# RWKV scratch sized to the chunk, four masked state buffers in place of one, and the MLP down-projection with the token block outside

## What is computed

```
layer 0: x += concat(pool_mixer, rwkv7(12 heads x 64)) @ ev_w_out
         x += square(relu(rmsnorm(x) @ ff_w1[0])) @ ff_w2[0]      # 1024 -> 4096 -> 1024
layer 1: x += concat(gmlp, rglru) @ od_w_out
         x += square(relu(rmsnorm(x) @ ff_w1[1])) @ ff_w2[1]
y = rmsnorm(x)
rwkv7 step, per head: S = S*w - (S kk)(kk*a)^T + v k^T ;  o = S r   # S is 64 x 64, carried
```

## Time and profile before

| | us |
|---|---|
| median of 2 runs | 5295.91 (5283.2 and 5308.62) |
| the profiled execution | 5305.1 |
| its span, slowest core (core 4) | 5303.5 |
| spans of the 8 cores | 5230.9 to 5303.5 |

### The profile page before, as it was taken

How to read it: one execution, slowest core, us unless ns; L and a number is a source line. 1 busy time by engine, 2 the same in 40 slices (tenths; PEclk the granted TensorE clock), 3 DMA queues, 4 the chain that set the end, 5 groups by cost and what they waited for, 6 DMA issues and landing times.

```text
span 5303.5 us, 107077 instructions; the slowest of 8 cores (5230.9 to 5303.5 us)
## 1 busy us (share of the span) xinstructions
PE 4604.0 (87%) x32575; PEld 3193.8 (60%) x32575; DVE 2754.5 (52%) x7970; ACT 1622.8 (31%) x4545; POOL 1426.1 (27%) x3000
## 2 busy tenths in 40 slices
PE   6898889988899888988897987999977787799998
PEld 5676666766677666766665763444456565544445
DVE  4645655556465564565552223666554544456664
ACT  2323333333233332333332112111144444321112
POOL 3313232232222322233211210333323232123320
PEclk8998899999999989888998788999989898899999
DMA  5031130221301313013023033222356555412211
GB/s 79 3 55 21 25 53 1 30 48 25 53 1 25 53 17 61 1 25 49 4 40 59 5 50 88 33 33 33 44 65 77 68 75 70 63 29 33 33 17 66
DMA packets 341496, 213.11 MB, mean 40 GB/s; under 512 B 34738, under 2 KB 326433, under 8 KB 339912
## 3 DMA queue, kind: packets, MB, share of 16 engines
q0 software_dynamic: 294704, 160.98, 23.6%
q1 hardware_dynamic: 46232, 45.28, 2.8%
HBM read 345.84 MB, written 21.35 MB: 69 GB/s over the span
## 4 chain that ended last, share of the span: by engine, by line
PE 58%; DVE 16%; issue 9%; DMA 8%; ACT 6%; POOL 1%; SPq 1%; DVEq 1%; ACTq 0%; POOLq 0%
PE psb L451 46%; PE psb L550 10%; DVE arena L418 6%; DVE arena_r L418 5%; ACT arena_r L434 3%; DVE arena L426 3%; PE psb L454 2%; ACT arena L434 2%; DMA arena<-od_w_in 2%; DMA arena<-xin 2%; DMA arena<-ev_w_in 2%; POOL arena L418 1%; DVE arena L423 1%; ACT L434 1%; DMA o_wkv_s<-arena 1%
## 5 line engine op out<-in xcount | busy, mean ns | idle before, releaser
L451 PE MATMUL psb<-arena 128*128 128x512 bf16 (+12 forms) x17296 | 2740.7, 314 | 446.5 <-DVE arena L426 126.9
L451 PEld LDWEIGHTS psb<-arena 128*128 128x128 bf16 (+4 forms) x17296 | 1655.1, 140 | 1393.0 <-issue 937.5
L550 PE MATMUL psb<-arena 128*128 128x256 bf16 x11359 | 1617.5, 286 | 6.9 <-DVE arena L442 6.9
L550 PEld LDWEIGHTS psb<-arena 128*128 128x128 bf16 x11359 | 1118.3, 103 | 300.9 <-issue 110.3
L418 POOL TENSOR_TENSOR arena<-arena 128x128 f32<-128x128 f32 (+5 forms) x1421 | 751.9, 547 | 1490.6 <-ACT arena L434 519.9
L434 ACT ACTIVATE arena<-psb 128x512 f32<-128x512 f32 (+7 forms) x900 | 369.2, 424 | 1917.7 <-PE psb L451 1485.0
L418 DVE TENSOR_TENSOR arena<-arena,psb 128x512 f32<-128x512 f32 (+2 forms) x1427 | 700.6, 564 | 432.4 <-PE psb L451 426.8
L434 ACT ACTIVATE arena<-arena 128x128 f32<-128x128 f32 (+7 forms) x1792 | 531.9, 331 | 727.3 <-PE psb L451 317.4
L418 DVE TENSOR_TENSOR arena_r<-arena_r,psb 128x256 fp32r<-128x256 f32 x1248 | 480.4, 418 | 434.0 <-ACT arena_r L434 428.8
L426 DVE SCALAR_TENSOR_TENSOR arena<-arena 128x128 f32<-128x128 f32 (+6 forms) x1138 | 417.8, 408 | 352.4 <-ACT arena L434 338.1
L442 DVE COPY arena<-psb 128x256 f32<-128x256 f32 (+7 forms) x663 | 243.9, 374 | 659.1 <-PE psb L451 280.4
(11 more groups left out here) (22 smaller groups left out, 1046.3 us busy)
## 6 DMA issues: line engine op xcount, KB each, us to landing
arena<-ev_w_in POOLq DMA_DIRECT2D x99, 512.0 KB, 11.1
arena<-od_w_in POOLq DMA_DIRECT2D x72, 512.0 KB, 10.9
arena<-ff_w POOLq DMA_DIRECT2D x64, 512.0 KB, 5.7
arena<-ev_w_out POOLq DMA_DIRECT2D x36, 512.0 KB, 8.3
arena<-od_w_out POOLq DMA_DIRECT2D x36, 512.0 KB, 16.1
arena<-xscr SPq DMA_DIRECT2D x8, 1056.0 KB, 14.7
arena<-xin SPq DMA_DIRECT2D x16, 512.0 KB, 8.0
xscr<-arena SPq DMA_DIRECT2D x64, 128.0 KB, 7.1
```

Source lines behind the costliest of these rows:

```text
L451: return self._op("pe", lambda e: e.matmul(out, lhsT, rhs, start=start, stop=stop), R, W, "mm", cost=cost, rows=rows)
L550: K.P.filler = lambda: K.P.make_filler(lambda e: e.matmul(f_out, f_l, f_r, start=True, stop=True), fdep)
```

## The change

Three edits. In `rwkv` the scratch tiles are as long as the chunk (`n`) and no longer 128 columns; for prompt chunks `n` is 128, so only the sample chunk (`n` = 64) differs. The sample chunk gets four buffers `UVm` that are used in turn. In the down-projection of the MLP the token block becomes the outer loop and the output tile the inner one.

```diff
@@ ffn_all
             wb2 = wtile(2, 1024, w2[c * 256:(c + 1) * 256, :].rearrange("(k p) c -> p k c", p=128))
-            for m in range(8):
-                for (t0, tn) in TBS:
+            for (t0, tn) in TBS:
+                for m in range(8):
                     ps = K.ps()
                     for k in range(2):
@@ rwkv
-        XS = [K.alloc(128) for _ in range(20)]
+        XS = [K.alloc(n) for _ in range(20)]
...
-        LP = [K.alloc(128) for _ in range(6)]
-        AR = [K.alloc(256) for _ in range(6)]
+        LP = [K.alloc(n) for _ in range(6)]
+        AR = [K.alloc(2 * n) for _ in range(6)]
...
-        X0T = K.alloc(256)
+        X0T = K.alloc(2 * n)
         X0 = K.alloc(256)
         Xs = K.alloc(256)
-        UVms = [K.alloc(512) for _ in range(1)] if sample else None
+        UVms = [K.alloc(512) for _ in range(4)] if sample else None
...
                 if nseq > 1:
-                    UVm = UVms[0]
+                    UVm = UVms[uvi[0] % 4]
                     uvi[0] += 1
```

More of the change, by code:

```diff
@@ L766, in rwkv @@
         esv = lambda q, c0, ln: K.arena[:, ES.off + q * 129: ES.off + q * 129 + nseq * Wd].rearrange("p (s w) -> p s w", w=Wd)[:, :, c0:c0 + ln]
-        dtmp = [K.alloc(128) for _ in range(8)]
+        dtmp = [K.alloc(n) for _ in range(8)]
         for q in range(20):
@@ L789, in rwkv @@
         Vv = XS[12:18]
-        TH = K.alloc(128)
-        SGg = K.alloc(128)
+        TH = K.alloc(n)
+        SGg = K.alloc(n)
         K.act(TH.ap(0, n, 0, 64), XS[18].ap(0, n, 0, 64), AF.Tanh, [XS[18]], [TH])
         K.act(SGg.ap(0, n), XS[19].ap(0, n), AF.Sigmoid, [XS[19]], [SGg])
-        LW = [K.alloc(128) for _ in range(6)]
-        Aa = [K.alloc(128) for _ in range(6)]
-        Gg = [K.alloc(128) for _ in range(6)]
+        LW = [K.alloc(n) for _ in range(6)]
+        Aa = [K.alloc(n) for _ in range(6)]
+        Gg = [K.alloc(n) for _ in range(6)]
         for j in range(6):
@@ L806, in rwkv @@
             K.cp("dve", Gg[j].ap(0, n), ps.ap(0, n), [ps], [Gg[j]])
[L807 to L811, removed]
+        KK = [K.alloc(n) for _ in range(6)]
+        KP = [K.alloc(n) for _ in range(6)]
+        BON = [K.alloc(n) for _ in range(6)]
+        t1 = [K.alloc(n) for _ in range(6)]
+        t2 = [K.alloc(n) for _ in range(6)]
         for j in range(6):
```

## The result

The changed kernel is slightly slower: its time is **1.0067** of the time before, 95% interval 1.0034 to 1.0099. On 5305 us that is some +35 us (+18 to +53). The forecast was +3. Its profiled execution took 5319.44 us with a span of 5317.9 on core 2. In some executions, whatever the kernel, the cores of a die run for hundreds of us at a granted clock of 0.81, a third level beside the two named ahead of the prediction; where a core's number can't be read without that, its clock stands beside it.

A forecast was written before the change was run, and what follows sets the result against it. TensorE's real work bounds the MLPs, a latency chain padded with fillers the sample state work. +60 (MLP order) - 57 (sample block) = +3 on 5305.1 gives 5308, less 9 for the runs' median: 5299 us, range 5270 to 5335.

The forecast's parts named there:

- The gate (+60): MLP down-projection: the new order makes the next up-projection start 1.88 us later in each of 32 chunks, costing 60 us.
- The bank argument: MLP: with seven rotating banks, the next up-projection must wait for the 34th of VectorE's 40 adds.
- "Clock 1.00" in the MLP: Both MLPs: a sign of the forecast being right, TensorE's granted clock staying at 1.00 with a period of 34.9 us.
- rival 2: MLPs: pauses drop the clock to 0.50 for a share s, costing 486 s us (49 at s = 0.1); chance 0.05.
- The sample block (-57): Sample state work: four mask buffers save 10.5 + 9.5 + 10.5 us in loops, 21.0 in preparations, 5.2 in stores.
- half way between the clock levels: Sample state loop: TensorE limits each step at 0.90 us, between 0.66 to 0.70 (high clock) and 1.10 to 1.18 (low).
- the prediction's own sum: Sample state loop, lower bound: all at the low clock, 12 x 1.14 + 8 x 0.24 = 15.6 us a loop.
- The stores (-5.2): Sample block: three intervals between stores 1 to 4 shrink from 19.2 to 14.0 us, a gain of 5.2.
- Shrunk scratch (0): Sample chunk's scratch tiles: no instruction changes and the tiles newly overlapped are read out long before, so no cost.
- Rival 1 (GpSimd): Sample state loop: GpSimd's scalings slow beside VectorE's masks, giving back up to 16 us in all, 5315 us; chance 0.20.
- Rivals 3 and 4: MLP gate is not the 34th add, 5239 us, chance 0.07; sample block's buffers do nothing, 5356 us, chance 0.06.

## Why the prediction was wrong

Point by point, by its own steps.

- **The gate (+60): right.** Forecast 34.9 us for a period and 19.7 us to the up-projection; measured 34.92 and 19.72 in the chunks at clock 1.00. Only the first period of each layer grew by less, 0.30 and not 1.88 (35.10 to 35.40 at clock 1.00), which makes 57 of the 60. The bank argument is borne out by moving the small block: last with either nesting 34.9 and 35.2, second 32.4.
- **"Clock 1.00" in the MLP: this step failed.** It stood in the list of what would show the forecast right, and its opposite was rival 2, with s = 0.1 and a chance of 0.05. The mechanism of rival 2 is what happens, at a small size: about half of the 32 chunks are 1.68 us longer, 14 x 1.68 = 24 us in all, which by its formula is s = 0.05. The evidence against it was read wrongly. In the kernel before TensorE goes at VectorE's pace for more than half of a chunk, but it doesn't stand idle there: it is busy for 31.30 of the 33.04 us. One small group at a time stands behind four large ones, and TensorE's rows between the waits are of ten large matmuls. The reorder gathers all eight small pairs in one place, at the very end of VectorE's backlog, where each waits for a large add: the prediction saw that wait and wrote of the fillers in it only that they cost nothing. It should have asked what TensorE does in those 4 us, and what the clock does behind them. The Trainium skill, "TensorE: Matmul & The Clock Gate", A second HAM failure mode: psum-queue depth-cycling, describes a clock that falls and rises because the engine idles briefly between groups. In the changed kernel the trace agrees (0.95 in the chunks of 36.6 us). In the kernel before, which cycles banks too and waits 0.38 us before pair after pair, it does not (1.00).
- **The sample block (-57): right in direction, -50 measured, and partly by luck.** By the earlier trace rows and the stretches above: the loops gave 9.5, 8.6 and 8.5 us where 10.5, 9.5 and 10.5 were taken; the preparations 14.6 and 13.2 where 10.5 each was taken, because fillers had taken 13.65 us of the first and take 3.16 now (63 and 14 of them in the trace), and its other matmuls 22.82 and 17.10 (280 and 232 on line 451, three steps' worth fewer and not two); the outputs cost 5.3 and 2.7 more, which was in no term. There the loop's first steps now stand among the output matmuls (x187 instead of x165) at a clock of 0.50 and 0.68, where it was 0.89 and 0.85. Sum: 26.6 + 27.8 - 8.0 = 46.4 on the two slowest cores; over all eight the piece that these stretches make up, from the first mask to the first store, is 48.5 shorter, where loops and preparations together were put at 51.5. The luck is in the loops: I took TensorE's pace half way between the clock levels, and the truth is the low one. At that level the prediction's own sum was 15.6 us a loop, and 13.05 to 14.10 were measured, because 64x64 matmuls in one long row take 0.062 us each, 0.99 for a step's 16, and not 1.14.
- **The stores (-5.2): right in size, not in place.** The timeline of the DMA queue on core 2, kernel before (first fence) and changed (second):

```profile
3101.34 78.95 SPq L465 DMA_DIRECT2D o_wkv_s<-arena  x16
```

```profile
3066.22 74.13 SPq L465 DMA_DIRECT2D o_wkv_s<-arena  x16
```

  Over the eight cores the 16 stores took 77.2 us before (74.3 to 78.9) and take 72.8 now (71.1 to 74.1): -4.4. But the three intervals between the first four stores, which the term named, are only 1.3 us shorter (16.0 to 14.7); on core 4, the one that the prediction read, they were 17.9, and 15.2 to 17.1 on the others. The other 3 us come in the stores behind, and why is not shown.
- **Shrunk scratch (0): probably some 3 to 4 us**, ahead of the first mask. The ratio of 1.0035, with 1 inside the interval, leaves a price of nothing open; the traces speak against it.
- **Rival 1 (GpSimd): it didn't happen.** The 32 scalings of a loop, which answer to the earlier trace rows, changed kernel:

```profile
2955.23 13.46 POOL L422 TENSOR_SCALAR arena<-arena 128x64 f32<-128x64 f32 x32 [29.85 <-PE psb L451]
```

  13.46 us and not 13.38, beside VectorE's 16 masks.
- **Rivals 3 and 4** are excluded by the period of 34.92 and by the sample stretch.
- **The sum.** +60 + 24 - 50 = +34 against +35 measured. The forecast missed by 24 for the clock and 7 for the sample block. That +35 still lies inside the prediction's own -30 to +42 is luck: its upper end is the gate at 62 less a sample block at 20, and holds nothing for the clock.

## What to carry to other kernels

When an order is changed, price a wait not only by its length but by what the engine does in it: a few us of small matmuls in front of a block of large ones can cost the large ones their clock, and this is seen in the granted clock of single periods, not in that of the stretch (0.98). Where output banks rotate, count which consumer stands seven groups ahead of the next stage and put the cheap ones before it: the small block second was worth 0.65 us a chunk, last it cost 1.9 to 3.6. And a filler is free only while TensorE waits, where it can even pay (without the seven of a chunk the typical period was 2.6 us longer than at clock 1.00): between small matmuls that follow each other closely it costs more than its own length.

## What was not expected of the hardware

- How often the clock falls depends on how much TensorE has to do in the waits: with no filler in each, all chunks (0.91, +2.6 us), with one, about half of them (0.95, +1.7), with four none on six of eight cores, and on the other two only chunks in a row at 0.81. Which chunks are hit with one filler is not told by anything in these traces.
- 64x64 f32 matmuls in a row take 0.062 us each at the lower clock, and the clock stays there though TensorE is busy all the time (13.05 of 13.05 us). Up to four fillers a step did not raise it. The kernel before had twelve a step and a clock of 0.89 to 0.95. How many it takes, and what the sample block would gain at the higher level, stays open.
- One filler of 256 columns between such matmuls costs 0.54 us at the lower clock. That it breaks their overlap is how I read the rows; no run took that apart.
